# One inference step of a hybrid RWKV-7 / attention trunk: the attention stage's order of work, and where two weight panels are split

## The reference, cut to what matters

```python
def swa_prompt(h, w_qkv, b_qkv, w_o, sink):
    q, k, v = qkv_proj(h, w_qkv, b_qkv, pos)       # 16 query heads, 4 key/value heads, 64 wide
    kw, vw = with_prev(kb), with_prev(vb)          # a block of 128 queries sees its own and the previous 128 keys
    scores = jnp.einsum('bnqkgd,bnskd->bnkgqs', qb, kw) * (HEAD_DIM ** -0.5)
    scores = jnp.where(mask[None, :, None, None], scores, -jnp.inf)
    probs = sink_softmax(scores, sink.reshape(KV_HEADS, GROUP))
    o = jnp.einsum('bnkgqs,bnskd->bnqkgd', probs, vw).reshape(B, S, ATT_HEADS * HEAD_DIM)
    return o @ w_o, k[:, S - w_keep:], v[:, S - w_keep:]
# then x = x + gate * (o @ w_o), a norm, and a squared-ReLU MLP (1024 -> 4096 -> 1024)
```

## Time and profile before

| | us |
|---|---|
| median of 3 runs | 3132.47 |
| the profiled execution | 3138.42 |
| its span | 3136.4 |
| PE busy in it, from the page | 2747.0 (88%) |
| attention stage, first PE instruction to last (1968.6 to 2254.3) | 285.7 |
| of it, ahead of the first scores | 43.7 |
| next stage, from the end of attention to continuous matmuls (2254.3 to 2275.6) | 21.3 |

### The profile page before, as it was taken

The page is one execution under the profiler, slowest core; times in us unless marked ns, Lnnn a source line. Parts: engine busy times, 40 slices in busy tenths (PEclk is TensorE's granted clock), DMA queues, the critical chain, the costliest instruction groups (busy, mean ns, idle before and its releaser), DMA issues. The chain is left out here.

```text
span 3136.4 us, 46946 instructions
## 1 busy us (share of the span) xinstructions
PE 2747.0 (88%) x19558; PEld 2568.7 (82%) x19558; DVE 1285.6 (41%) x2275; ACT 946.1 (30%) x1795; POOL 599.2 (19%) x374
## 2 busy tenths in 40 slices
PE   5497868967885789999999999798689999999998
PEld 3366868866774689999999999777588999999998
DVE  3443677335886572122121235366455212122223
ACT  2254633222222453121120234355434213021221
POOL 0011111112334202212122130210110222222130
PEclk8698989988997799999999999899789999999999
DMA  6665767756562612222222231401030111111121
GB/s 235 219 253 189 223 195 241 214 148 133 110 125 91 206 57 101 82 74 94 89 74 81 88 92 50 115 20 38 25 97 21 48 45 44 48 47 48 48 68 55
DMA packets 375917, 331.87 MB, mean 106 GB/s; under 512 B 109878, under 2 KB 345082, under 8 KB 368652
## 3 DMA queue, kind: packets, MB, share of 16 engines
q1 hardware_dynamic: 353564, 286.32, 30.6%
q0 software_dynamic: 7488, 26.39, 2.3%
q10 hardware_dynamic: 14672, 16.39, 1.8%
HBM read 248.92 MB, written 78.78 MB: 104 GB/s over the span
## 5 line engine op out<-in xcount | busy, mean ns | idle before, releaser
L706 POOL TENSOR_TENSOR wL<-raw,wH 128x1024 fp32r<-128x1024 f32 x120 | 288.4, 2404 | 1306.5 <-ACT wH L825 1306.5
L727 PE MATMUL t_acc<-oneH,wH 128*128 128x344 f32 x1440 | 465.2, 323 | 5.8 <-DVE oneL L1041 4.4
L728 PE MATMUL t_acc<-oneL,wH 128*128 128x344 f32 x1440 | 461.1, 320 | 0.0
L729 PE MATMUL t_acc<-oneH,wL 128*128 128x344 f32 x1440 | 461.0, 320 | 0.0
L727 PE MATMUL t_acc<-twoH,wH 128*128 128x344 f32 x1392 | 449.2, 323 | 7.0 <-DVE twoL L1041 4.7
L728 PE MATMUL t_acc<-twoL,wH 128*128 128x344 f32 x1392 | 445.7, 320 | 0.0
L729 PE MATMUL t_acc<-twoH,wL 128*128 128x344 f32 x1392 | 445.6, 320 | 0.0
L991 DVE SCALAR_TENSOR_TENSOR X<-t_acc,mod,X 128x344 f32<-128x344 f32 (+1 forms) x240 | 137.4, 572 | 611.0 <-PE t_acc L729 601.5
L1064 DVE TENSOR_TENSOR t_g<-t_g 128x344 f32<-128x344 f32 x192 | 99.4, 517 | 554.7 <-ACT t_g L845 554.7
L727 PEld LDWEIGHTS t_acc<-oneH,wH 128*128 128x128 f32 x1440 | 271.2, 188 | 19.3 <-issue 10.1
L825 ACT ACTIVATE wH<-raw 128x1024 fp32r<-128x1024 f32 x120 | 126.5, 1054 | 508.6 <-PE t_acc L729 508.6
(11 more groups left out here) (455 smaller groups left out, 5154.5 us busy)
## 6 DMA issues: line engine op xcount, KB each, us to landing
raw<-in_mlp_down SPq DMA_DIRECT2D x64, 512.0 KB, 3.8
raw<-in_mlp_up SPq DMA_DIRECT2D x62, 512.0 KB, 4.1
ada_ring<-in_ada_w SPq DMA_DIRECT2D x24, 1024.0 KB, 9.7
t_shared<-in_ada_w SPq DMA_DIRECT2D x24, 1024.0 KB, 6.3
kvrb_hx<-hx_saved ACTq DMA_DIRECT2D x16, 516.5 KB, 4.1
kvr_work<-scr_L SPq DMA_DIRECT2D x16, 516.0 KB, 4.7
X<-x_saved SPq DMA_DIRECT2D x6, 1376.0 KB, 6.9
raw<-in_at_wqkv SPq DMA_DIRECT2D x12, 512.0 KB, 4.0
```

Of the source, the lines that this page charges most:

```text
L706: pool.tensor_tensor(low, raw[:, w % 2], high.bitcast(F32), ALU.subtract).then_inc(s_low, 1)
L727: pe.matmul(out, high[:, k, :], h[:, k, third[t]], start=(k == 0), stop=False)
L728: pe.matmul(out, high[:, k, :], l[:, k, third[t]], start=False, stop=False)
L729: return pe.matmul(out, low[:, k, :], h[:, k, third[t]], start=False, stop=(k == DB - 1))
```

## The change

In the attention stage:

1. In each step PE makes `scores(n + 2)` ahead of `turn(n)` (with the samples' work rearranged around them; ACT's `turned(n)` goes behind `cache_turned`).
2. Eight units instead of six come before the first scores, and `k_rows` (the key rows for the output) after unit 5 instead of unit 3. `units_before` then gives one unit each to k = 0: t = 0 to 3, 6, 7; k = 1: t = 0 to 3, 6, 7; k = 2: t = 0 to 3. The ropes and the `low` splits move a step forward with them.
3. Panels o0 and o1 are split in this stage, into `wH` and `wL` (`high(8)`, `high(9)`, `low(8)`, `low(9)`), in steps 16 and 19; SP no longer waits for their loads at the end.

In the tail of layer 1: the first two units read those; SP's first two loads (o2, o3) wait for nothing; `high` and `low` of o0 and o1 are gone; u0 and u1 are split in third 2 instead of third 1, since o0 and o1 hold their slots to the end of their last units (16 and 17); two loads of X move in SP's queue from panels 9 and 11 to 8 and 9.

```diff
+            if kind == "o" and p < HERE:
+                return [x[:, p] for x in (wH, wL)]
...
             def weights(w):
-                if w >= 2:
-                    sp.wait_ge(s_low, w - 1)
+                if w >= HERE + 2:
+                    sp.wait_ge(s_low, w - 1 - HERE)
...
-                if layer == 1 and w in (5, 9, 11):
+                if layer == 1 and w in (5, 8, 9):
...
-            high(0)
-            high(1)
+            if layer == 0:
+                high(0)
+                high(1)
...
-                    if t == 1 and p in (3, 5):
+                    if t == 1 + layer and p in (3, 5):
                         high(DB + p // 2 - 1)
...
         def units_before(n):
-            if n == 0:
-                return (6, 7)
             k, t = group(n)
-            if t == TILES - 1 and k < LAST - 1:
-                return (6 * k + 12,)
-            return (6 * k + 7 + t,) if k < LAST and t <= 4 else ()
+            if t >= TILES - 2 and k < LAST - 1:
+                return (6 * k + 6 + t,)
+            return (6 * k + 8 + t,) if k < LAST and t <= 3 else ()
...
-            for u in range(6):
+            for u in range(8):
                 unit(u)
-                if u == 3:
+                if u == 5:
                     k_rows()
...
                 if n:
                     values(n - 1)
-                turn(n)
+                if n + 2 < STEPS:
+                    scores(n + 2)
                 if two:
                     sample_scores(two[0])
                     turn_cache(two[1])
-                if n + 2 < STEPS:
-                    scores(n + 2)
+                turn(n)
                 if two:
                     sample_scores(two[1])
...
-                if k < LAST and t in (2, 5):
-                    rope(2 * k + 4 + t // 5)
-                if k < LAST and t == 5:
+                if k < LAST and t in (1, 4):
+                    rope(2 * k + 4 + t // 4)
+                if k < LAST and t == 4:
                     queries(k + 1)
```

More of the change, by code:

```diff
@@ L668, in _ @@
                 weights(w)
-                if layer == 1 and w in (5, 9, 11):
-                    t = (5, 9, 11).index(w)
+                if layer == 1 and w in (5, 8, 9):
+                    t = (5, 8, 9).index(w)
                     sp.wait_ge(s_pl, (t + 1) * DB)
@@ L703, in _ @@
             for w, (kind, p) in enumerate(panels):
-                pool.wait_ge(s_high, w + 1)
+                if w < HERE:
+                    continue
+                pool.wait_ge(s_high, w + 1 - HERE)
                 high, low = place(kind, p)
@@ L740, in unit @@
                 kind, p, t = order[u]
-                pe.wait_ge(s_low, number[kind, p] + 1)
+                if number[kind, p] >= HERE:
+                    pe.wait_ge(s_low, number[kind, p] + 1 - HERE)
                 if u >= 4:
@@ L816, in high @@
                     act.wait_ge(s_early[w % 2], 16 * (w // 2 + 1))
-                elif w >= HERE:
+                else:
                     act.wait_ge(s_raw[w % 2], 16 * ((w - EARLY - HERE) // 2 + 1))
@@ L822, in high @@
                         act.wait_ge(s_done, last_unit[ring[r - 2]] + 1)
+                    elif layer == 1:
+                        act.wait_ge(s_done, last_unit["o", r] + 1)
                 elif kind in ("d", "kv"):
@@ L1083, in tile_out @@
                     dve.wait_ge(s_fg, 16)
-                    dve.wait_ge(s_low, len(panels))
+                    dve.wait_ge(s_low, len(panels) - HERE)
                 dve.wait_ge(s_froot, i + 1)
@@ L2809, in _ @@
             sp.wait_ge(s_out, 96)
-            for s in range(2):
-                sp.wait_ge(s_raw[s], 16 * (DB // 2))
         @block.gpsimd
@@ L2843, in _ @@
                     sink(n + 2)
-                if k < LAST and t in (1, 4) and 2 * k + 4 + t // 4 < DB:
-                    low(2 * k + 4 + t // 4)
+                if k < LAST and t in (0, 3) and 2 * k + 4 + t // 3 < DB + 2:
+                    low(2 * k + 4 + t // 3)
+            pool.wait_ge(s_low, DB)
             pool.wait_ge(s_ks, 2)
@@ L3011, in evict @@
                 act.activation(Q[:, p % 4, third[t]], bank[:, 0:TT], ACT.Identity, bias=net.param[:, at + p:at + p + 1]).then_inc(s_q, 1)
-                if t == NT - 1 and p + 2 < DB:
+                if t == NT - 1:
                     high(p + 2)
@@ L3070, in _ @@
                     out(n - 1)
-                turned(n)
                 if two:
                     cache_turned(two[1])
+                turned(n)
                 if (k, t) == (LAST, 4):
```

## The result

| | before | after |
|---|---|---|
| median of the runs, us | 3132.91 (3128.95 to 3135.44) | 3108.19 (3104.67 to 3111.13) |
| ratio | | 0.9922, 95% interval 0.9905 to 0.9939 |
| profiled execution / span | 3138.42 / 3136.4 | 3109.05 / 3107.0 |
| attention stage, from PE's first instruction to the first on DVE behind PE's last | 285.7 | 266.1 |
| from the end of attention to the eighth block of the next stage's first unit, on PE | 22.37 | 22.80 |

The change makes the kernel 24.7 us faster; predicted was 22.6. The total hides two errors that nearly cancel: attention gave more than predicted, and the start of the next stage gave nothing.

The account below looks back on a forecast made before the run. PE, busy 88% of the span, was taken to bound unit steps, and a loop through DVE plain steps. Attention 13.9, tail start 3.0 and u0/u1 5.7 sum to 22.6 us off 3132.5: 3109.9 us, range 3101 to 3121.

Parts of the forecast that it names:

- Ahead of the first scores: Before the attention steps: SP issues panel 1's partner rows earlier, so the first scores come 1.8 us sooner.
- Step 0: First attention step: one unit instead of two, 4.5 us less, bounds 3.8 to 6.
- k = 0 and k = 1: Attention step groups 0 and 1: one free plain step each loses the scores from its loop, 2.2 us less together.
- k = 2: Attention step group 2: step 20 becomes plain (2.6 us), steps 22 and 23 win some 0.8; 3.4 us less.
- Steps 24 to 27: Attention steps with sample work: turn takes the scores' place in an equally long loop, 6.90 us a step; change 0.
- rival 1: PE's clock better than now in steps 24 to 27, in step 0 and at 2344: 3104 us; chance 13%.
- Steps 28 and 29: Attention steps without sample work: the scores leave the loop in both, 2.0 us less.
- o0 and o1 split in attention: Steps 16 and 19: ACT copies and POOL splits hidden in unit steps, cost 0; 2.1 us if that cover went.
- Start of the tail: After attention: o2 and o3 load earlier and the chain behind moves along, 3.0 us less (1.5 to 3.5).
- u0 and u1 moved: Tail: splits in third 2 instead of third 1 remove a 5.7 us delay that PE pays; 5.7 us less.
- rival 3: Moved splits delay norms ahead of the up panels: 3116 us, or 3118 with the tail's start held by loads; chance 10%.
- Rival 2: PE's clock worse in serial steps: plain steps lose their 1.1 us gain, sample steps up to 3; 3118 us; chance 12%.

Follow-up runs that it names:

- the pair: The two profiled executions, one of the kernel before and one of the changed kernel; 3138.42 and 3109.05 us.
- order_only: Kernel before with only the scores put ahead of turn, ACT's `turned` behind the second cache's copy; 3122.4 us, ratio 0.9960.
- attention_only: Changed kernel's attention stage without the splits of o0 and o1, the stage after it as in the kernel before; 3110.6 us, ratio 0.9928.
- one_load: Changed kernel, but at the start of the last stage the load of o3 waits for ACT's copy of o2; 3103.1 us, ratio 0.9900.
- blocks_first: Changed kernel, but in the last stage ACT makes all eight attention-output blocks' high parts ahead of its copies of o2 to o5; 3098.5 us, ratio 0.9886.
- up_third2: Kernel before with u0 and u1 split in third 2 instead of third 1 and two X loads moved; 3127.3 us, ratio 0.9974.
- early_and_blocks: blocks_first with o2 and o3 also loaded in the attention stage; 3098.4 us, ratio 0.9891.
- x_first: early_and_blocks with the first X load ahead of o4 and o5, and ACT's copies of o6 and o7 behind units 1 and 3; 3101.3 us, ratio 0.9906.

## Why the prediction was right, and where it was wrong

The total, the sign and the range were right. By its own steps, with the pair and, where several kernels share the code, their spread:

- *Ahead of the first scores, -1.8*: -1.5 in the pair; the nine kernels with eight units ahead have m0 of 43.1 to 44.3, the three others 45.0 to 46.7. Right. The wait at the first scores was foreseen as under 6 us and is 4.2 to 5.8. Not foreseen: unit 6 waited 2.0 us for panel 2's low part ("long made", the text said), in the shade of the rope.
- *Step 0, -4.5*: -5.6, within the bounds of 3.8 to 6. Of it 0.5 is the scores' place (order_only), which the term left out.
- *k = 0 and k = 1, -2.2*: -5.0 (2.9 and 2.1). Less than half of it was forecast. Two reasons can be named. The term "in unit steps PE is full either way: 0" was wrong by 0.17 us a step, as order_only shows. And unit 12 in k = 0 had run at a low clock (5.25 us) and now ran at the full one (4.01). No edit did that, and in k = 1 it went the other way: unit 18 took 4.4 us before and 5.5 now. A plain step gained 1.02 for the 1.1 of the forecast.
- *k = 2, -3.4*: -3.2. Right.
- *Steps 24 to 27, 0*: -1.0 in the pair, up to -4.9 in the other kernels with that order. The text took the loop as equally long in both orders, with 1.09 in the place of 1.13. At full clock it is 0.95 us shorter over the four steps, which is all that the pair gained, since its low clock cost the same on both sides (4.0 and 3.9). What the other kernels gained beyond that is the clock; the bound given for it was 4.0, and rival 1 had it.
- *Steps 28 and 29, -2.0*: -3.3 to the end of the stage in the pair. From mask 29 to the end the seven kernels with the new order throughout take 25.8 to 28.6 us for 28.9 to 29.9.
- *o0 and o1 split in attention, 0*: right. attention_only has the stage without them, 267.4 us for 266.1.
- *Start of the tail, -3.0*: **wrong**: +0.4 at the eighth block, +1.5 where the matmuls become continuous (the 21.3 us of the table before), between 0 and +1.4 at mean 1, about 0 at the end. The step that failed is "everything behind is a chain of load, copy, low part, load, so it moves by the 3.45 us, less some for two 512 KB loads". The first link did move by 3.5. But the chain had been staggered by the old start, one panel every 3.5 us with two blocks between; the two loads now land as a pair, their two splits stand back to back on POOL, the next two loads wait for these, and DVE can pass one block per POOL split. I had read the collision (2.40 for 0.52) and used it for u0 and u1, but not here, where the same pair meets twice. one_load shows that it is the pairing: with the loads of o2 and o3 apart, and so o2's split alone on POOL, 2.3 us of the 3.0 are there at mean 1. What pairs of splits cost is read from the trace of after (6.50 us from o4's copy to the eighth block for 4.94) and was not tested apart from the loads. blocks_first shows the place from the other side: with the blocks out of the chain, 10 us come free.
- *u0 and u1 moved, -5.7*: -5.6 in the pair (mean 1 to mean 2, 39.0 us to 33.4), -5.5 alone in up_third2. Right in size and place. That the collision would only change its payer (rival 3) did not come: the waits at the up panels stayed 4.4 and 4.5.

So attention gave 19.6 in the pair for 13.9, the tail's start 3 less than forecast, the move of u0 and u1 what it should. That 22.6 came so near to 24.7 is in part luck: terms left out in attention and an error in the tail had opposite signs.

Rival 2 (a worse clock in the serial steps) is not in the pair, whose plain step ran at full clock, but it is real: in attention_only, blocks_first, early_and_blocks and x_first a plain step took 5.96 us at a granted clock of 0.73 to 0.75, for 6.10 in the kernel before, so that nearly all the gain of that step was gone.

## What to carry to other kernels

Two instructions on one engine that feed different consumers should stand in the order in which data can be there, not in pairs by design: in this case eight 0.4 us block copies, six of them behind panel copies that waited for 5 us loads, cost 10 us of a 3100 us kernel, more than a third of what the whole change brought. Taking away a wait at the head of a chain is worth what the last link moves, so follow it to the instruction that PE waits for and ask whether the links now arrive together. And where two engines exclude each other on a port, look for every place where they meet, not only for the one where it was first seen.

## What the runs showed that was not expected

The same code gets different clocks: from mask 24 to mask 29 the new order had a granted clock of 0.71 to 0.95 and took 31.5 to 35.4 us, and mask 1 to mask 24 took 158.9 to 164.8 us at a mean of 0.92 to 0.98 in the kernels built on the change. With what lies ahead (the stage starts between 1960.5 and 1968.6 us) this is the spread of single executions, and it is as large as half of the parts of this change. A part of 3 us was to be had from the trace, by stretches measured from the same event, and not from medians of four or five runs.

A unit's first matmul starts 0.24 us before the end of the transposes ahead of it and 0.07 before that of the scores, which have 64 rows of weights at a time. What in the scores makes the difference wasn't tried.

Of the kernels with more changes the one with the blocks first (3098.5 us, 0.9886, interval 0.9871 to 0.9901) beats both that the case began with beyond the intervals. No run tells those built on it from it.
